# Forget gates' logits and softplus: from the front of the softmax attention into the last chunk of the input projection

## The chip, the cores and the metric

The kernel runs on one core of one Trainium2 chip. The metric is the device time of one execution in microseconds; the median of several runs counts. A core has five engines that run their own instruction queues in order and meet through semaphores: TensorE (matrix products and transposes, into the eight banks of PSUM), VectorE, ScalarE, GpSimd and SyncE, which here starts nearly all DMA transfers.

## The reference, cut to what matters

Two layers of one transformer block (the first block) are followed by one layer of another, on 512 tokens of width 1024 in float32. The change touches the first block's attention, which runs twice. For each layer:

```python
h = rms_norm(x, attn_pre_g[l])
proj = h @ w_in[l]                      # 1024 -> 3080 columns
qa, ka, va, qb, kb, vb, f_logit = jnp.split(proj, split_at, axis=-1)   # 6 x 512 and 8 columns
...                                     # rotary on qa, ka; differential attention on qa, ka, va
log_f = jax.nn.log_sigmoid(f_logit.astype(f32) + forget_bias[l].astype(f32))
ob = forgetting_attention(qb, kb, vb, log_f)
# in it: c = jnp.cumsum(log_f, axis=1); logits = q k / 8 + (c_q - c_k), causal softmax, times v
```

log_sigmoid(y) is computed as min(y, 0) - ln(1 + exp(-|y|)). The 8 columns f_logit are the "logits" of this document, ln(1 + exp(-|y|)) its softplus, and c its running sums.

## The kernel before, in words

**Number format.** A float32 product is made of three fp32r matmuls: operands are split into a rounded part (`_hi`) and the rest (`_lo`), and `three` (lines 1793 to 1797) issues hi x hi, hi x lo and lo x hi. ScalarE rounds each 1024 x 512 piece of weights (`hi_lap`, line 742), GpSimd subtracts to get the rest (`lo_lap`, line 649), and SyncE loads the raw piece (line 547). A weight chunk is 1024 rows by 512 columns, held in four slots of 256 rows (r = 0 to 3). TensorE counts the semaphore `w_used` up when it is through with a slot; ScalarE may then write the next chunk's rounded weights there.

**The input projection.** The stage is named `in0` or `in1` after its layer and has six chunks of 512 output columns: qa, ka, va, qb, kb, vb. Chunk c writes banks 0 to 3 of PSUM when c is even and banks 4 to 7 when it is odd. One slot of one chunk is 2 x 4 x 3 = 24 matmuls of 512 columns (`use_slot` in `token_chunk`). VectorE copies each finished chunk out of PSUM (line 1341, chunk 5 at line 1339) and counts `evac[c % 2]` up, on which TensorE waits before it writes these banks again. On TensorE chunks 0 and 1 are straight code; chunks 2 to 5 are a hardware loop of two passes over two chunks each (`pe.Fori` in `project`, line 1948).

**The front of the attention** (`attention1`, one function of this name on ScalarE, line 859, VectorE, line 1332, and TensorE, line 2040). TensorE's order is: the 16 logit matmuls (lines 2046 and 2047, 16 stationary columns: the 8 forget columns' rounded part and rest) into bank 0, once chunk 4 has been copied out; the wait for chunk 5's copy (`evac[1]`); then 16 items of four 128 x 128 transposes each (line 2037), which turn the heads' q and k and use banks 2 to 7 in rotation. Items with an even number are taken out of PSUM by ScalarE (line 854), those with an odd one by VectorE (line 1371), and an item waits for the one that stood in its bank six items earlier. Between items 1 and 2 TensorE turns the logits back to tokens on partitions, with four small transposes (line 2056) into bank 1, after ScalarE has copied them from bank 0 (line 867). VectorE adds the bias and the two parts (lines 1364 and 1365) ahead of item 3, ScalarE does Abs, Exp and Ln (lines 872 to 874) ahead of item 4, and VectorE makes the gate (line 1368) ahead of item 9. After item 15 TensorE waits for the last items on both engines and for the gate, then makes the running sums (lines 2067 and 2069) and begins with the attention's score products (line 2102).

**What sets the order.** Everything is written out by hand: each engine's queue is in the order of the code, and semaphores tie them. ScalarE's queue at this place is: the rounding of the six chunks' weights, the rounding of the out projection's first four slots (`hi_first(f"out{l}")`, each waits for chunk 5 to be through with the slot), the copy of the logits, and then the items.

Of the kernel before, what the change touches and what calls it, by code (L numbers as in the profile page):

```python
# [170 lines left out]
def build(nc, x, positions, attn_pre_g, w_in, forget_bias, lam_q1, lam_k1, lam_q2, lam_k2, diff_sub_g,  # L171
# [4 lines left out]
    with ctx:  # L176
# [545 lines left out]
        def _(act):  # L722
# [3 lines left out]
            def link(ins):  # L726

                steps[0] += 1
                ins.then_inc(act_step, 1)
                act.wait_ge(act_step, steps[0])  # L730
# [13 lines left out]
            def hi_first(stage, slots=range(R)):  # L744

                hi_lap(stage, LAP0[stage], 0, FFN_SEEN.get(stage), slots)
# [112 lines left out]
            def attention1(l):  # L859
                stage = f"in{l}"  # L860

                with act.Fori(2 if l == 0 else 1, LAPS[stage]) as lap:
                    hi_lap(stage, LAP0[stage] + lap)
                hi_first(f"out{l}")

                act.wait_ge(f_mm, l + 1)
                nc.scalar.activation(f_rows, PS[0:16, 0, :], ACT.Copy).then_inc(f_copied, 1)

                for n, item in enumerate(items1):
                    if n == 4:  # L870
                        act.wait_ge(f_biased, l + 1)
                        link(nc.scalar.activation(fy[:, 1], fy[:, 0], ACT.Abs))
                        link(nc.scalar.activation(fy[:, 1], fy[:, 1], ACT.Exp, scale=-1.0))
                        nc.scalar.activation(fy[:, 1], fy[:, 1], ACT.Ln, bias=1.0).then_inc(f_log, 1)
                    if n % 2 == 0:
                        act.wait_ge(tr_mm, len(items1) * l + n + 1)
                        turned_out(item, 2 + n % 6).then_inc(tr_act, 1)
# [296 lines left out]
        def _(dve):  # L1174
# [157 lines left out]
            def attention1(l):  # L1332
                stage = f"in{l}"
                dst = (QA, KA, VA, QB, KB, None)
                for c in range(6):
                    chunk_done(stage, c)
                    src = banks(c % 2)
# [22 lines left out]
                for n, (src, rows, to, scale) in enumerate(items1):  # L1360
                    if n == 3:
                        dve.wait_ge(f_turned, l + 1)
                        parts = PS[:, 1, 0:T * 16].rearrange("p (t h) -> p t h", h=16)
                        link(V.tensor_tensor(fy[:, 0], parts[:, :, 0:8], fbias[:, l, :].unsqueeze(1).to_broadcast([P, T, 8]), ALU.add))
                        V.tensor_tensor(fy[:, 0], parts[:, :, 8:16], fy[:, 0], ALU.add).then_inc(f_biased, 1)
                    if n == 9:
                        dve.wait_ge(f_log, l + 1)
                        V.scalar_tensor_tensor(fy[:, 2], fy[:, 0], 0.0, fy[:, 1], ALU.min, ALU.subtract).then_inc(f_gate, 1)
                    if n % 2:
                        dve.wait_ge(tr_mm, len(items1) * l + n + 1)  # L1370
                        V.tensor_scalar(to, PS[0:rows, 2 + n % 6, :], scale, None, ALU.mult).then_inc(tr_dve, 1)
# [418 lines left out]
        def _(pe):  # L1790
# [96 lines left out]

            def token_chunk(stage, lap, s, laps, first, next_stage=None, tiled=False):

# [4 lines left out]
                for lap3 in range(laps):  # L1894
                    for r, subs in enumerate(lap_subs(stage, lap3)):
# [3 lines left out]
                        for sub in range(subs):  # L1899
# [7 lines left out]
                            if sub == subs - 1:  # L1907
                                last.then_inc(w_used, 1)
                            if first and not is_down(stage):
                                transposed_next(stage, k)  # L1910
# [19 lines left out]
                for r in range(R):  # L1930
# [6 lines left out]
                    last.then_inc(w_used, 1)  # L1937

            def project(stage):

                n = LAPS[stage]
                for c in range(2):
# [3 lines left out]
                    else:  # L1946
                        token_chunk(stage, LAP0[stage] + c, c, 1, c == 0)
                with pe.Fori(1, n // 2) as i:
                    for s in range(2):
                        pe.wait_ge(evac[s], SET0[stage][s] + i)  # L1950
                        token_chunk(stage, LAP0[stage] + 2 * i + s, s, 1, False)
                if n % 2:
# [87 lines left out]
            def attention1(l):  # L2040
                stage = f"in{l}"

                pe.wait_ge(evac[0], SET0[stage][0] + 3)
                pe.wait_ge(fw_done, 1)
                for k in range(KD):
                    mm(PS[0:16, 0, :], fw[:, l, k, :], xt_hi[:, k, :], start=k == 0, stop=False)
                    last = mm(PS[0:16, 0, :], fw[:, l, k, :], xt_lo[:, k, :], start=False, stop=k == KD - 1)
                last.then_inc(f_mm, 1)
                pe.wait_ge(evac[1], SET0[stage][1] + 3)
                base = len(items1) * l  # L2050
                for n in range(8):
                    if n == 2:

                        pe.wait_ge(f_copied, l + 1)
                        for t in range(T):
                            last = nc.tensor.transpose(PS[:, 1, 16 * t:16 * t + 16], f_rows[:, t * P:(t + 1) * P],
                                                       ident[0:16, 0:16])
                        last.then_inc(f_turned, 1)
                    transpose_item(n, base, items1, 2 + n % 6, 6)
                for n in range(8, len(items1)):  # L2060
                    transpose_item(n, base, items1, 2 + n % 6, 6)
# [326 lines left out]
```

## Time and profile before

| what | value |
|---|---|
| three runs | 2107.34 us median, 2105.56 to 2108.14 |
| the profiled execution's own time | 2107.81 us |
| its span, first to last instruction | 2106.0 us |
| granted TensorE clock, mean | 0.997 |
| TensorE busy | 2061.6 us, 98% of the span |
| VectorE busy | 1146.7 us, 54% |
| ScalarE busy | 915.1 us, 43% |
| GpSimd busy | 598.2 us, 28% |

The busy time of an engine is the time in which it has an instruction in work; TensorE's matmuls overlap each other, so that the start of one to the start of the next is the time that a matmul costs in a row of them, and the duration shown for one is longer than that. The profile is of one execution, and times in its rows count from its first instruction.

### The profile page before, as it was taken

To read this page: it belongs to the slowest core of one execution; us is meant where nothing else is said; L and a number is where in the kernel's file an instruction comes from. 1 tells how busy PE (TensorE), PEld (TensorE's weight loads), DVE (VectorE), ACT (ScalarE), POOL (GpSimd) and SP (SyncE) were. 2 spreads that over 40 slices of the span, in tenths; PEclk is the share of its full clock that TensorE was granted. 3 is DMA by queue.
4 is the path that set the end of the run, shared out by engine and by line. 5 is a ranking of instruction groups with operands and counts; after the bars stand their busy time and mean duration, and the time that the engine had idled before them with its cause. 6 is when DMAs were issued, how large, how long until landed. Compare 5 with 4: busy or idle time off the path is not lost.

```text
span 2106.0 us, 31405 instructions
## 1 busy us (share of the span) xinstructions
PE 2061.6 (98%) x12462; PEld 1795.2 (85%) x12462; DVE 1146.7 (54%) x1784; ACT 915.1 (43%) x1556; POOL 598.2 (28%) x438
## 2 busy tenths in 40 slices
PE   7999999999999999999999999999999999999999
PEld 6886789999887886789999887877788889999987
DVE  6417558776305117558776306477566445877700
ACT  4226454455324126454455325455534434545611
POOL 3540030000544440030000543444466441000252
PEclk9999999999999999999999999999999999999999
DMA  5330023332323330023332331211211232333232
GB/s 193 100 110 1 2 90 104 98 121 91 112 94 98 98 100 1 1 90 103 99 120 91 110 95 55 82 59 50 61 51 51 101 100 81 101 101 111 86 114 72
DMA packets 129143, 178.80 MB, mean 85 GB/s; under 512 B 10163, under 2 KB 78062, under 8 KB 129006
## 3 DMA queue, kind: packets, MB, share of 16 engines
q1 hardware_dynamic: 128414, 175.24, 26.3%
q8 instruction: 96, 1.57, 0.3%
q10 hardware_dynamic: 592, 1.64, 0.2%
q14 instruction: 41, 0.34, 0.1%
HBM read 174.76 MB, written 2.10 MB: 84 GB/s over the span
## 4 chain that ended last, share of the span: by engine, by line
PE 42%; issue 42%; POOL 7%; DVE 6%; ACT 2%; DMA 0%; POOLq 0%; DVEq 0%; ACTq 0%
PE PS L1795 10%; PE PS L1797 10%; PE PS L1796 10%; POOL w_lo L649 7%; PE PS L2127 2%; PE PS L2102 2%; PE PS L2247 1%; PE PS L2086 1%; DVE nmax L1403 1%; PE PS L2037 1%; PE PS L2223 1%; PE PS L2215 1%; PE PS L1849 1%; PE PS L2109 0%; DVE R L1413 0%
## 5 line engine op out<-in xcount | busy, mean ns | idle before, releaser
L649 POOL TENSOR_TENSOR w_lo<-R,w_hi 128x1024 fp32r<-128x1024 f32 x168 | 404.4, 2416 | 1184.9 <-ACT w_hi L742 1125.7
L1795 PE MATMUL PS<-w_hi,xt_hi 128*128 128x512 f32 x928 | 375.3, 404 | 10.6 <-DVE R L1604 4.3
L1795 PE MATMUL PS<-xt_hi,w_hi 128*128 128x256 f32 (+1 forms) x1216 | 367.3, 302 | 0.0
L742 ACT ACTIVATE w_hi<-R 128x1024 fp32r<-128x1024 f32 (+1 forms) x180 | 183.4, 1029 | 423.2 <-PE PS L1797 422.8
L1797 PE MATMUL PS<-w_hi,xt_lo 128*128 128x512 f32 x928 | 364.3, 393 | 0.0
L1796 PE MATMUL PS<-w_lo,xt_hi 128*128 128x512 f32 x928 | 363.5, 392 | 0.0
L1797 PE MATMUL PS<-xt_hi,w_lo 128*128 128x256 f32 (+1 forms) x1216 | 361.8, 298 | 0.0
L1796 PE MATMUL PS<-xt_lo,w_hi 128*128 128x256 f32 (+1 forms) x1216 | 361.6, 297 | 0.0
L1796 PEld LDWEIGHTS PS<-xt_lo,w_hi 128*128 128x128 f32 x1216 | 233.0, 192 | 6.9 <-issue 1.0
L1795 PEld LDWEIGHTS PS<-xt_hi,w_hi 128*128 128x128 f32 x1216 | 233.0, 192 | 7.0 <-issue 1.0
L1797 PEld LDWEIGHTS PS<-xt_hi,w_lo 128*128 128x128 f32 x1216 | 232.9, 192 | 6.5
L1795 PEld LDWEIGHTS PS<-w_hi,xt_hi 128*128 128x128 f32 x928 | 175.5, 189 | 48.4 <-issue 6.8
L1795 PE MATMUL PS<-w_hi,ht_hi 128*128 128x512 f32 x528 | 206.5, 391 | 1.2 <-POOL w_lo L649 0.8
L1797 PEld LDWEIGHTS PS<-w_hi,xt_lo 128*128 128x128 f32 x928 | 175.2, 189 | 37.7
L1796 PE MATMUL PS<-w_lo,ht_hi 128*128 128x512 f32 x528 | 205.7, 390 | 0.0
L1797 PE MATMUL PS<-w_hi,ht_lo 128*128 128x512 f32 x528 | 205.6, 389 | 0.0
L1796 PEld LDWEIGHTS PS<-w_lo,xt_hi 128*128 128x128 f32 x928 | 175.8, 189 | 33.7 <-issue 1.0
L1484 DVE TENSOR_TENSOR w_lo<-UF,w_hi 128x1024 fp32r<-128x1024 f32 x108 | 131.9, 1221 | 52.3 <-ACT w_hi L950 52.3
L633 POOL TENSOR_TENSOR w_lo<-raw,w_hi 128x256 fp32r<-128x256 f32 x160 | 119.7, 779 | 118.3 <-ACT w_hi L1030 75.0
L950 ACT ACTIVATE w_hi<-UF 128x1024 fp32r<-128x1024 f32 x108 | 113.2, 1051 | 29.4 <-PE PS L1797 29.4
L1797 PE MATMUL PS<-UR,w_lo 128*128 128x256 f32 x432 | 122.4, 283 | 0.0
L1796 PE MATMUL PS<-UR,w_hi 128*128 128x256 f32 x432 | 122.4, 283 | 0.0
(299 smaller groups left out, 3546.2 us busy)
## 6 DMA issues: line engine op xcount, KB each, us to landing
R<-in_w_in SPq DMA_DIRECT2D x56, 512.0 KB, 3.8
R<-in_w_down SPq DMA_DIRECT2D x40, 512.0 KB, 3.4
UW<-in_w_gate SPq DMA_DIRECT2D x36, 512.0 KB, 4.0
UW<-in_w_up SPq DMA_DIRECT2D x36, 512.0 KB, 5.0
raw<-in_w_in SPq DMA_DIRECT2D x36, 512.0 KB, 3.7
R<-in_w_out SPq DMA_DIRECT2D x24, 512.0 KB, 3.3
R<-in_w_ffn_down SPq DMA_DIRECT2D x20, 512.0 KB, 3.4
UW<-in_w_ffn_gate SPq DMA_DIRECT2D x18, 512.0 KB, 4.0
```

Of the source, the lines that this page charges most:

```text
L633: last = nc.gpsimd.tensor_tensor(w_lo[:, r, n // 2, cols], raw[:, r, n // 2, cols], w_hi[:, r, n // 2, cols].bitcast(F32), ALU.subtract)
L649: nc.gpsimd.tensor_tensor(w_lo[:, r, 0:subs, :], raw_of(stage, lap)[:, r, 0:subs, :], w_hi[:, r, 0:subs, :].bitcast(F32), ALU.subtract).th ...
L742: nc.scalar.activation(w_hi[:, r, 0:subs, :], raw_of(stage, lap)[:, r, 0:subs, :], ACT.Copy).then_inc(hi_ready, 1)
L950: nc.scalar.activation(slot_hi[slot], src, ACT.Copy).then_inc(u_hi, 1)
L1403: V.tensor_reduce(nmax[:, bank:bank + 2], PS[:, bank:bank + 2, 0:P * (i + 1)], AX.X, ALU.max, negate=True).then_inc(max_done, 2)
L1484: V.tensor_tensor(slot_lo[slot], src, slot_hi[slot].bitcast(F32), ALU.subtract).then_inc(u_lo, 1)
L1795: mm(out_, a_hi, b_hi, start=start, stop=False, **kw)
L1796: mm(out_, a_hi, b_lo, start=False, stop=False, **kw)
L1797: return mm(out_, a_lo, b_hi, start=False, stop=stop, **kw)
L1849: last = nc.tensor.transpose(PS[:, half_bank(stage, half, k), a:a + P], SOURCE[stage][:, 2 * half + t, k * P:(k + 1) * P], ident[:, :])
L2102: mm(PS[:, u % 4 + m, 0:upto], q[halves[m], pair, upto - P:upto], kk[halves[m], pair, 0:upto], start=True, stop=False)
L2127: last = mm(PS[:, 6 + n % 2, 0:width], probT[:, n % 2, j * P:(j + 1) * P], vals, start=j == 0, stop=j == i)
```

## The change

The same instructions are issued in another order, with one loop of TensorE written out.

- TensorE: the logit matmuls and the small transposes become functions of their own (`forget_logits`, `forget_turned`). `token_chunk` gets an argument `between`, which calls them behind slot 1 and behind slot 2 of chunk 5. For this chunks 2 to 5 of both input projections are straight code instead of a loop. `attention1` begins with the wait for chunk 5's copy and issues the 16 items without interruption.
- ScalarE: the copy of the logits and Abs, Exp and Ln stand ahead of the rounding of the out projection's first four slots, and no longer behind it and among the items.
- VectorE: bias, sum and gate stand ahead of the wait for chunk 5, and no longer among the items.
- The running sums stay behind the items.

```diff
@@ -861,17 +861,15 @@
 
                 with act.Fori(2 if l == 0 else 1, LAPS[stage]) as lap:
                     hi_lap(stage, LAP0[stage] + lap)
-                hi_first(f"out{l}")
-
                 act.wait_ge(f_mm, l + 1)
                 nc.scalar.activation(f_rows, PS[0:16, 0, :], ACT.Copy).then_inc(f_copied, 1)
+                act.wait_ge(f_biased, l + 1)
+                link(nc.scalar.activation(fy[:, 1], fy[:, 0], ACT.Abs))
+                link(nc.scalar.activation(fy[:, 1], fy[:, 1], ACT.Exp, scale=-1.0))
+                nc.scalar.activation(fy[:, 1], fy[:, 1], ACT.Ln, bias=1.0).then_inc(f_log, 1)
+                hi_first(f"out{l}")
 
                 for n, item in enumerate(items1):
-                    if n == 4:
-                        act.wait_ge(f_biased, l + 1)
-                        link(nc.scalar.activation(fy[:, 1], fy[:, 0], ACT.Abs))
-                        link(nc.scalar.activation(fy[:, 1], fy[:, 1], ACT.Exp, scale=-1.0))
-                        nc.scalar.activation(fy[:, 1], fy[:, 1], ACT.Ln, bias=1.0).then_inc(f_log, 1)
                     if n % 2 == 0:
                         act.wait_ge(tr_mm, len(items1) * l + n + 1)
                         turned_out(item, 2 + n % 6).then_inc(tr_act, 1)
@@ -1333,6 +1331,13 @@
                 stage = f"in{l}"
                 dst = (QA, KA, VA, QB, KB, None)
                 for c in range(6):
+                    if c == 5:
+                        dve.wait_ge(f_turned, l + 1)
+                        parts = PS[:, 1, 0:T * 16].rearrange("p (t h) -> p t h", h=16)
+                        link(V.tensor_tensor(fy[:, 0], parts[:, :, 0:8], fbias[:, l, :].unsqueeze(1).to_broadcast([P, T, 8]), ALU.add))
+                        V.tensor_tensor(fy[:, 0], parts[:, :, 8:16], fy[:, 0], ALU.add).then_inc(f_biased, 1)
+                        dve.wait_ge(f_log, l + 1)
+                        V.scalar_tensor_tensor(fy[:, 2], fy[:, 0], 0.0, fy[:, 1], ALU.min, ALU.subtract).then_inc(f_gate, 1)
                     chunk_done(stage, c)
                     src = banks(c % 2)
                     if c == 5:
@@ -1358,14 +1363,6 @@
                         rotary(dst[c])
 
                 for n, (src, rows, to, scale) in enumerate(items1):
-                    if n == 3:
-                        dve.wait_ge(f_turned, l + 1)
-                        parts = PS[:, 1, 0:T * 16].rearrange("p (t h) -> p t h", h=16)
-                        link(V.tensor_tensor(fy[:, 0], parts[:, :, 0:8], fbias[:, l, :].unsqueeze(1).to_broadcast([P, T, 8]), ALU.add))
-                        V.tensor_tensor(fy[:, 0], parts[:, :, 8:16], fy[:, 0], ALU.add).then_inc(f_biased, 1)
-                    if n == 9:
-                        dve.wait_ge(f_log, l + 1)
-                        V.scalar_tensor_tensor(fy[:, 2], fy[:, 0], 0.0, fy[:, 1], ALU.min, ALU.subtract).then_inc(f_gate, 1)
                     if n % 2:
                         dve.wait_ge(tr_mm, len(items1) * l + n + 1)
                         V.tensor_scalar(to, PS[0:rows, 2 + n % 6, :], scale, None, ALU.mult).then_inc(tr_dve, 1)
@@ -1885,7 +1882,7 @@
                         if half == 1:
                             last.then_inc(w_used, 1)
 
-            def token_chunk(stage, lap, s, laps, first, next_stage=None, tiled=False):
+            def token_chunk(stage, lap, s, laps, first, next_stage=None, tiled=False, between=None):
 
                 a_hi, a_lo = (ht_hi, ht_lo) if is_down(stage) else (xt_hi, xt_lo)
                 kn = KF if is_down(stage) else KD
@@ -1906,6 +1903,8 @@
                                             k == 0, k == kn - 1)
                             if sub == subs - 1:
                                 last.then_inc(w_used, 1)
+                                if between and r in between:
+                                    between[r]()
                             if first and not is_down(stage):
                                 transposed_next(stage, k)
                             k += 1
@@ -1936,6 +1935,23 @@
                     last = tile_product(3, r, k0[r], k0[r] == 0)
                     last.then_inc(w_used, 1)
 
+            def forget_logits(l):
+
+                pe.wait_ge(evac[0], SET0[f"in{l}"][0] + 3)
+                pe.wait_ge(fw_done, 1)
+                for k in range(KD):
+                    mm(PS[0:16, 0, :], fw[:, l, k, :], xt_hi[:, k, :], start=k == 0, stop=False)
+                    last = mm(PS[0:16, 0, :], fw[:, l, k, :], xt_lo[:, k, :], start=False, stop=k == KD - 1)
+                last.then_inc(f_mm, 1)
+
+            def forget_turned(l):
+
+                pe.wait_ge(f_copied, l + 1)
+                for t in range(T):
+                    last = nc.tensor.transpose(PS[:, 1, 16 * t:16 * t + 16], f_rows[:, t * P:(t + 1) * P],
+                                               ident[0:16, 0:16])
+                last.then_inc(f_turned, 1)
+
             def project(stage):
 
                 n = LAPS[stage]
@@ -1945,10 +1961,11 @@
                         chunk_by_half(stage, 0)
                     else:
                         token_chunk(stage, LAP0[stage] + c, c, 1, c == 0)
-                with pe.Fori(1, n // 2) as i:
-                    for s in range(2):
-                        pe.wait_ge(evac[s], SET0[stage][s] + i)
-                        token_chunk(stage, LAP0[stage] + 2 * i + s, s, 1, False)
+                l = int(stage[-1])
+                for c in range(2, n):
+                    pe.wait_ge(evac[c % 2], SET0[stage][c % 2] + c // 2)
+                    hooks = {1: lambda: forget_logits(l), 2: lambda: forget_turned(l)} if c == n - 1 else None
+                    token_chunk(stage, LAP0[stage] + c, c % 2, 1, False, between=hooks)
                 if n % 2:
                     set_free(stage, n - 1, 0)
                     token_chunk(stage, LAP0[stage] + n - 1, 0, 1, False)
@@ -2040,24 +2057,9 @@
             def attention1(l):
                 stage = f"in{l}"
 
-                pe.wait_ge(evac[0], SET0[stage][0] + 3)
-                pe.wait_ge(fw_done, 1)
-                for k in range(KD):
-                    mm(PS[0:16, 0, :], fw[:, l, k, :], xt_hi[:, k, :], start=k == 0, stop=False)
-                    last = mm(PS[0:16, 0, :], fw[:, l, k, :], xt_lo[:, k, :], start=False, stop=k == KD - 1)
-                last.then_inc(f_mm, 1)
                 pe.wait_ge(evac[1], SET0[stage][1] + 3)
                 base = len(items1) * l
-                for n in range(8):
-                    if n == 2:
-
-                        pe.wait_ge(f_copied, l + 1)
-                        for t in range(T):
-                            last = nc.tensor.transpose(PS[:, 1, 16 * t:16 * t + 16], f_rows[:, t * P:(t + 1) * P],
-                                                       ident[0:16, 0:16])
-                        last.then_inc(f_turned, 1)
-                    transpose_item(n, base, items1, 2 + n % 6, 6)
-                for n in range(8, len(items1)):
+                for n in range(len(items1)):
                     transpose_item(n, base, items1, 2 + n % 6, 6)
                 pe.wait_ge(tr_act, (base + len(items1)) // 2)
                 pe.wait_ge(tr_dve, (base + len(items1)) // 2)
```

## Rows read from the trace of the kernel before

**Rows 1.** The page, part 1: busy us (share of the span) and instructions.
```profile
PE 2061.6 (98%) x12462; PEld 1795.2 (85%) x12462; DVE 1146.7 (54%) x1784; ACT 915.1 (43%) x1556; POOL 598.2 (28%) x438
```

**Rows 2.** Waits of TensorE, whole span: us in total, times, longest.
```profile
PE PS L2067 <- ACT R L854: 1.7, 2, 0.8
```

**Rows 3.** Timeline of layer 0: start us, us, engine, line, what, count [idle before <-releaser].
```profile
149.63 0.39 PE L1797 MATMUL PS<-w_hi,xt_lo 128*128 128x512 f32 x1
...
150.06 2.29 DVE L1339 COPY R<-PS 128x2048 f32<-128x2048 f32 x1 [19.47 <-PE PS L1797]
...
151.25 2.40 POOL L649 TENSOR_TENSOR w_lo<-R,w_hi 128x1024 fp32r<-128x1024 f32 x1 [3.04 <-ACT w_hi L742]
...
153.33 0.39 PE L2047 MATMUL PS<-xt_lo,fw 128*16 128x512 f32 x1
...
153.56 1.03 PE L2037 MATMUL PS<-ident,R 128*128 128x128 f32 x8
153.76 0.59 ACT L867 ACTIVATE R<-PS 16x512 f32<-16x512 f32 x1 [2.58 <-PE PS L2047]
...
154.53 0.42 PE L2056 MATMUL PS<-ident,R 16*128 16x16 f32 x4
...
154.88 6.33 PE L2037 MATMUL PS<-ident,R 128*128 128x128 f32 x56
155.25 0.18 DVE L1364 TENSOR_TENSOR fy<-PS,fbias 128x32 f32<-128x32 f32 x1
...
156.06 0.22 ACT L872 ACTIVATE fy<-fy 128x32 f32<-128x32 f32 x1
...
158.36 0.18 DVE L1368 SCALAR_TENSOR_TENSOR fy<-fy 128x32 f32<-128x32 f32 x1
...
161.25 0.69 DVE L1371 TENSOR_SCALAR R<-PS 128x512 f32<-128x512 f32 x1 [0.18 <-PE PS L2037]
...
162.04 0.38 PE L2067 MATMUL PS<-fy,sums_r 128*128 128x32 f32 x2 [0.83 <-ACT R L854]
```

**Rows 4.** The same timeline at the same place of layer 1.
```profile
781.53 0.39 PE L1797 MATMUL PS<-w_hi,xt_lo 128*128 128x512 f32 x1
...
781.96 2.29 DVE L1339 COPY R<-PS 128x2048 f32<-128x2048 f32 x1 [19.47 <-PE PS L1797]
...
785.47 1.04 PE L2037 MATMUL PS<-ident,R 128*128 128x128 f32 x8
```

**Rows 5.** Timeline at the loop's back edge, chunk 3 to chunk 4, layer 0.
```profile
106.11 0.39 PE L1797 MATMUL PS<-w_hi,xt_lo 128*128 128x512 f32 x1
...
106.34 0.39 PE L1795 MATMUL PS<-w_hi,xt_hi 128*128 128x512 f32 x1
...
106.54 2.29 DVE L1341 COPY R<-PS 128x2048 f32<-128x2048 f32 x1 [17.55 <-PE PS L1797]
```

**Rows 6.** Timeline: matmuls that follow transposes within a projection's chunk.
```profile
651.02 0.48 PE L1795 MATMUL PS<-w_hi,xt_hi 128*128 128x512 f32 x1
...
651.34 0.39 PE L1796 MATMUL PS<-w_lo,xt_hi 128*128 128x512 f32 x1
```

**Rows 7.** Stretches: length, busy us (instructions) of each engine, PEclk, DMA share, GB/s.
```profile
153.50:162.00 8.50, 7.71 (x69) 7.21 (x67) 5.92 (x11) 5.71 (x12) 0.16 (x1) 1.00 0.20 64
...
164.70:168.10 3.40, 3.40 (x12) 1.41 (x12) 2.18 (x6) 1.89 (x8) 0.00 (x0) 0.50 0.00 0
...
1506.10:1512.90 6.80, 4.99 (x14) 3.55 (x13) 4.50 (x3) 1.59 (x2) 4.84 (x4) 0.50 0.00 0
...
640.00:646.00 6.00, 4.66 (x25) 3.67 (x25) 2.67 (x8) 4.94 (x10) 4.57 (x2) 1.00 0.26 86
```

**Rows 8.** Timeline of TensorE at three places behind idle time.
```profile
9.45 1.94 PE L1849 MATMUL PS<-ident,R 128*128 128x128 f32 x8 [4.24 <-DVE R L1202]
...
643.82 1.09 PE L1849 MATMUL PS<-ident,R 128*128 128x128 f32 x8 [1.34 <-DVE R L1202]
...
1505.45 0.50 PE L1795 MATMUL PS<-w_hi,xt_hi 128*128 128x512 f32 x1 [2.03 <-DVE R L1604]
```

## The prediction, made before the changed kernel was run

> **What bounds the kernel now.** I read the busy shares on the page first. TensorE is busy for 2061.6 of 2106.0 us, so a change earns time only if it shortens TensorE's instruction stream or its waits [rows 1]. The second view is TensorE's table of waits. At the place of the change it knows one kind of wait only: 1.7 us over both layers, at the running sums on line 2067, for the last turned head pair to leave PSUM (it names ScalarE; the timeline shows VectorE's evacuation ending last) [rows 2]. The third view, the timeline, gives the order of the work around it in layer 0 [rows 3]. Behind the projection's last matmul (start 149.63) TensorE goes straight on with the 16 forget-logit matmuls, the last of which starts at 153.33, and then with the first 8 transposes at 153.56. Under the logits, and this is the row to look at, VectorE copies chunk 5 out of PSUM from 150.06 to 152.35. The transposes wait for that copy, but it has been over for 1.2 us when they are due, so the wait costs nothing. Layer 1 repeats this to within 0.01 us [rows 4], so every cost below counts twice.
>
> **The change part by part.**
>
> *Logits moved ahead of slots 2 and 3.* The 16 matmuls cost (153.56 - 149.63 - 0.23) = 3.70 us of TensorE, 0.23 us each, at either place; the matmuls next to them are also 0.23 us apart [rows 3, 5]. Their work is neither added nor removed. The two waits that come with them are over before: bank 0 was copied out under chunk 5's first slot (chunk copies take 2.29 us, a slot is 24 matmuls of 0.227 = 5.4 us), and the converted forget weights date from the start of the kernel. In layer 0 the logits now stand 10.9 us ahead of the chunk's end.
>
> *What they covered is bare.* Chunk 5's last matmul is now the last thing before the head pairs' transposes, which still wait for chunk 5's copy. The copy starts 0.43 us behind the start of the last matmul (150.06 - 149.63) and lasts 2.29 us. TensorE restarts 0.10 us behind such a release (161.25 + 0.69 = 161.94 to 162.04) or 0.18 us (ScalarE's 153.76 + 0.59 = 154.35 to 154.53); I take 0.14 [rows 3]. From last matmul to first transpose that is 0.43 + 2.29 + 0.14 = 2.86 us, where now one step of 0.23 us stands between two instructions. So TensorE loses 2.63 us in each layer. Bounds: 2.59 and 2.67 us. Nothing else is in TensorE's queue that could pass this wait, since it is ahead of all the transposes on an in-order queue.
>
> *Turned logits moved between slots 2 and 3.* In the kernel before they interrupt the transposes: 8 transposes of 0.109 us would end 0.87 us behind 153.56, and the next run starts at 154.88, so the interruption with its wait for ScalarE's copy costs 1.32 - 0.87 = 0.45 us. At the new place ScalarE has 5.4 us for its 0.59 us copy, so the wait is gone; the four small transposes are 0.35 us, and a matmul behind transposes takes 0.32 us to its successor and not 0.23 (651.02 to 651.34) [rows 3, 6]. 0.35 + 0.09 = 0.44: nothing gained, between 0 and 0.1 us per layer either way.
>
> *Bias, Abs, Exp, Ln and the gate.* They run on VectorE and ScalarE. From the last small transpose (about 154.8) to the end of Ln about 2.0 us pass now (biases at 155.25, three ScalarE steps of 0.25 us from 156.06), with a head pair's evacuation in between. At the new place that chain and the gate (0.18 us) need some 2 us and have slot 3's 5.4 us as cover. VectorE is then back at its wait for chunk 5 with over 3 us to spare; without the cover each microsecond of lateness would be one of TensorE. Taking them out of the transposes gives nothing: those run at TensorE's own step, 56 in 6.10 us, and the running sums wait for the last evacuation (161.94), not for the gate, which was ready at 158.54 [rows 3]. That 0.83 us wait stays as it is and is what comes late next.
>
> *ScalarE's roundings of the out projection's first weights* now queue behind Ln. Three of 1.06 us fit between Ln and the end of the chunk or just behind it, while ScalarE has no transpose to evacuate for 2.9 us. GpSimd's four subtractions of 2.40 us bunch behind them and run over the copy and the transposes. In the trace one of them already lies over chunk 5's copy from 151.25, and that copy took the 2.29 us of the others [rows 3, 5]: no charge. SyncE's four loads of the next weights wait for those subtractions and start up to 10 us later; their data are needed only behind the attention, which begins then. No charge.
>
> *Loop unrolled.* TensorE's loop over chunks 2 to 5 becomes straight code. Its back edge lies between the matmuls at 106.11 and 106.34, where chunk 3's copy (106.54) shows the chunk's end. The step is 0.23 us as everywhere, so nothing is saved here [rows 5]. The Trainium skill, "Runtime: NRT & Kernel Launch", section "Instruction fetch mechanics", says that a taken branch to a target outside the fetched window stalls the engine until it is loaded, and prefers unrolling. By that rule unrolling would gain; the row at the back edge shows no stall, so its sum stands only among the rivals.
>
> *TensorE's clock.* The granted clock was 1.00 in the whole of 153.50:162.00, though TensorE did nothing but transposes there. It was 0.50 (1.2 GHz) in 1506.10:1512.90, behind a wait of 2.03 us, and in 164.70:168.10, behind the 0.83 us wait and small matmuls; an idle stretch of 1.34 us at 643.82 left it at 1.00 [rows 7, 8]. The new idle stretch (about 2.5 us) is nearest to the one of 2.03 us, so a fall is to be expected in part of the executions. At the lower level 8 transposes take 1.94 us and not 1.09 [rows 8], about double per step. A stretch as long as the 3.40 us of 164.70:168.10 at half speed loses 1.7 us of transposes at most, and less where it begins while TensorE still waits. Bounds for the two layers: 0 and 3.4 us; I take the middle, 1.7 us.
>
> **The sum.** 2 x 2.63 = 5.3 us of bare copy, 0 for the rest, 1.7 us for the clock: +7.0 us. The profiled execution took 2107.81 us (span 2106.0 and 1.8 around it), which gives 2114.8; it lies 0.47 us above the median of the runs shown, 2107.34, so the forecast for a median is 2114.3. Its own range is 2107.34 + 4.7 to + 8.9 with half a microsecond either way for the spread of the runs: 2111.6 to 2116.7.
>
> **The rivals.**
>
> 1. *The clock does not come back under transposes.* All 64 transposes of each layer run at 1.2 GHz: 64 x (0.213 - 0.109) = 6.7 us per layer, 13.3 in all, 2107.34 + 5.3 + 13.3 = 2125.9. For it: no row shows the clock rising while TensorE only transposes; the 8 at 9.45 stay low. Against it: 8.5 us of transposes kept the high level [rows 7]. The Trainium skill, "TensorE: Matmul & The Clock Gate", Part 4, says that transposes do not count as busy for the clock in the same way; the kept level at 153.50:162.00 speaks against its strong form. 10%.
>
> 2. *The other side: the loop was paid for after all.* If entry and back edge of the loop cost TensorE time that the modelled starts do not show, unrolling returns it: 4 such places (two layers, entry and back edge). To come out within 0.2% (4.2 us) it must return over 2.8 us of the 7.0, 0.7 us each, as much as the larger waits of this stage; to make the kernel faster by over 0.2% it must return 11.2 us, 2.8 us each. From 1.75 us each the change is no longer slower at all: 2107.3. For it: only the rule of the Trainium skill named above. Against it: the 0.23 us step at the back edge [rows 5]. 10%, of which 3% for faster.
>
> 3. *The chain is late.* If the gate's chain took more than slot 3 (5.4 us), VectorE's copy of chunk 5 would start late and TensorE wait longer still. The chain would have to be 3.4 us longer than the trace shows, as when ScalarE is held by something queued ahead of it; a microsecond behind that is 2 us over both layers, so about 2118. Against it: ScalarE's queue is empty there once chunk 5's weights are rounded. 5%.
>
> **How the numbers follow.** The forecast has 75%, the rivals 10, 10 and 5. A measurement of this kernel tells about 0.2%, 4.2 us, from no change. The forecast's low end of +4.2 touches that, where a copy is released a little earlier or the before kernel's median lies higher on the measuring chip: 3 of its 75 count as "same", with 7 of rival 2. Faster 0.03, same 0.10, slower 0.87. The range reaches down into rival 2 and up to rival 3: 2110.6 to 2118.5; rival 1 and most of rival 2 stay outside.
>
> **What would show it.** In the changed kernel's timeline a wait of TensorE on VectorE's chunk-5 copy (line 1339 before) of 2.4 to 2.6 us ahead of the first head pair, in both layers; the logits in the middle of chunk 5 with steps of 0.23 us around them; no wait for the turned logits; Ln ended before chunk 5's last matmul; the wait at the running sums unchanged at 0.8 us; GpSimd over the first transposes and no VectorE evacuation longer than 0.69 us; and the granted clock just behind the new wait, 1.00 or 0.50. The prediction is wrong if no such wait appears, if the transposes take longer than 7 us at a clock of 1.00, or if something else than this stage moves.

## The result and the profile after

The changed kernel takes 2113.61 us in the median of 8 runs (2112.12 to 2115.46), the kernel before 2107.03 us in 8 runs beside it (2105.34 to 2108.14). The ratio is 1.0034, with a 95% interval of 1.0025 to 1.0043: 6.6 us slower, where 7.0 us slower was forecast (2114.3, 2110.6 to 2118.5). The profiled execution took 2115.11 us.

Part 1 of the changed kernel's page answers to [rows 1].

```profile
PE 2062.7 (98%) x12462; PEld 1796.1 (85%) x12462; DVE 1147.0 (54%) x1784; ACT 915.1 (43%) x1556; POOL 597.7 (28%) x438
```

TensorE has the same 12462 matmuls and only 1.1 us more busy time, in a span that is 6.7 us longer. So the time is mostly idling. TensorE's table of waits has one entry that [rows 2] do not know, and the old one beside it, unchanged (us in total, times, longest):

```profile
PE PS L2054 <- DVE R L1344: 4.8, 2, 2.4
...
PE PS L2069 <- ACT R L854: 1.7, 2, 0.8
```

Line 2054 holds the items' transposes and line 1344 chunk 5's copy. The timeline of layer 0 shows the place; it answers to [rows 3].

```profile
147.96 0.39 PE L1794 MATMUL PS<-w_hi,xt_lo 128*128 128x512 f32 x1
148.27 0.41 PE L1951 MATMUL PS<-ident,R 16*128 16x16 f32 x4
148.62 0.50 PE L1792 MATMUL PS<-w_hi,xt_hi 128*128 128x512 f32 x1
148.73 0.19 DVE L1337 TENSOR_TENSOR fy<-PS,fbias 128x32 f32<-128x32 f32 x1 [18.09 <-PE PS L1951]
...
148.95 0.40 PE L1793 MATMUL PS<-w_lo,xt_hi 128*128 128x512 f32 x1
...
149.70 0.23 ACT L869 ACTIVATE fy<-fy 128x32 f32<-128x32 f32 x1
149.84 2.94 ACT L742 ACTIVATE w_hi<-R 128x1024 fp32r<-128x1024 f32 x3
...
150.96 9.36 POOL L649 TENSOR_TENSOR w_lo<-R,w_hi 128x1024 fp32r<-128x1024 f32 x4 [19.08 <-ACT w_hi L742]
...
153.99 0.39 PE L1794 MATMUL PS<-w_hi,xt_lo 128*128 128x512 f32 x1
154.41 2.29 DVE L1344 COPY R<-PS 128x2048 f32<-128x2048 f32 x1 [4.26 <-PE PS L1794]
154.47 1.06 ACT L742 ACTIVATE w_hi<-R 128x1024 fp32r<-128x1024 f32 x1 [1.69 <-PE PS L1794]
156.76 8.87 PE L2054 MATMUL PS<-ident,R 128*128 128x128 f32 x64 [2.38 <-DVE R L1344]
...
157.89 0.69 DVE L1368 TENSOR_SCALAR R<-PS 128x512 f32<-128x512 f32 x1 [1.19 <-PE PS L2054]
...
166.46 0.38 PE L2069 MATMUL PS<-fy,sums_r 128*128 128x32 f32 x2 [0.83 <-ACT R L854]
```

The chain of the logits is over early: Ln ends at 149.93 and VectorE is back at its wait for chunk 5 4.3 us before that is due. What follows the last projection matmul (153.99) is the copy alone, and TensorE stands until 156.76. The same place of layer 1 answers to [rows 4]:

```profile
791.08 2.29 DVE L1344 COPY R<-PS 128x2048 f32<-128x2048 f32 x1 [4.26 <-PE PS L1794]
...
793.43 7.21 PE L2054 MATMUL PS<-ident,R 128*128 128x128 f32 x64 [2.38 <-DVE R L1344]
```

The wait is the same, but the 64 transposes take 8.87 us in layer 0 and 7.21 us in layer 1. The table of stretches names the reason (length, busy us of TensorE, its weight loads, VectorE, ScalarE, GpSimd, granted clock, DMA share, GB/s); it answers to [rows 7].

```profile
156.80:157.80 1.00, 1.00 (x10) 1.00 (x10) 0.00 (x0) 0.35 (x1) 1.00 (x1) 1.00 0.86 182
157.90:161.30 3.40, 3.40 (x18) 3.40 (x17) 1.53 (x3) 1.34 (x3) 2.42 (x2) 0.50 0.66 243
161.40:165.60 4.20, 4.20 (x39) 4.00 (x37) 3.20 (x5) 2.75 (x5) 0.00 (x0) 1.00 0.36 125
168.20:171.50 3.30, 3.30 (x14) 1.69 (x14) 1.76 (x5) 1.77 (x8) 0.00 (x0) 0.50 0.02 5
...
793.40:800.50 7.10, 7.07 (x64) 6.97 (x64) 4.84 (x7) 4.45 (x8) 3.61 (x2) 1.00 0.67 222
```

In layer 0 the granted clock was 0.50 (1.2 GHz) for 3.4 us from 1.1 us behind the end of the wait, and fell again in the attention's first products; in layer 1 it did neither. It was back at 1.00 (2.4 GHz) with nothing but transposes on TensorE. From start to start a transpose took 0.213 us at 0.50 and 0.109 us at 1.00; 16 of them fell into the low stretch, which makes 16 x 0.104 = 1.66 us.

The start of an execution shifts by up to 1.5 us from one to the next, so times of two traces are compared from a mark. The mark here is the last transpose that feeds the projection (32.77 and 664.68 in the kernel before). Starts behind it, in us, read off the timelines of the profiled executions; the rows below the second are kernels of the experiments further down:

| kernel | first item, both layers | running sums, layer 0 / 1 | first transpose of the out projection, layer 0 / 1 |
|---|---|---|---|
| before | 120.79 | 129.27 / 129.27 | 212.71 / 212.85 |
| changed | 123.94 | 133.64 / 131.97 | 217.49 / 214.72 |
| loop written out | 120.79 | 129.27 / 129.26 | 213.01 / 211.99 |
| 10 matmuls in the wait | 123.94 | 131.98 / 131.97 | 214.72 / 214.72 |
| two items ahead | 121.40 | 131.10 / 131.10 | 213.84 / 213.83 |
| four items ahead | 121.40 | 130.23 / 130.24 | 212.97 / 212.99 |
| copy twice | 126.26 | 136.55 / 136.44 | 219.31 / 219.18 |
| only TensorE's part | 123.94 | 133.64 / 133.63 | 216.38 / 216.35 |
| before, sums first | 120.80 | 128.29 / 128.27 | 211.05 / 211.02 |
| four items and sums first | 121.40 | 129.24 / 129.23 | 212.03 / 212.02 |
| before, wait filled | 120.79 | 129.27 / 129.26 | 212.03 / 212.02 |

Without a clock fall the running sums start 2.70 us later than before (131.97 against 129.27), with one 4.37 us. From the sums to the out projection it is 82.75 us without a fall (changed kernel, layer 1) and 83.4 to 83.9 with one; the kernel before had one in both layers of its profile. So the two profiles differ by 4.78 us in layer 0 and by 1.87 us in layer 1, 6.65 in all, and under 0.2 us is left for the rest of the kernel. That this agrees with the 6.6 us of the medians is in part chance: the profiled executions had clock falls that many others did not have, as is counted behind the experiments.

### The profile page after: what moved, and what is told of

Same layout as the page of the kernel before. It is cut to its first block, busy times and chain, and to the rows that moved or that the text cites. A ratio compares the mean times of both kernels' runs of the same rounds, so it can differ in the third digit from the quotient of the medians.

```text
span 2112.7 us, 31367 instructions
## 1 busy us (share of the span) xinstructions
PE 2062.7 (98%) x12462; PEld 1796.1 (85%) x12462; DVE 1147.0 (54%) x1784; ACT 915.1 (43%) x1556; POOL 597.7 (28%) x438
## 4 chain that ended last, share of the span: by engine, by line
PE 42%; issue 41%; POOL 7%; DVE 7%; ACT 2%; DMA 0%; POOLq 0%; DVEq 0%; ACTq 0%
PE PS L1792 10%; PE PS L1794 10%; PE PS L1793 10%; POOL w_lo L649 7%; PE PS L2129 2%; PE PS L2104 2%; PE PS L2249 1%; PE PS L2088 1%; DVE nmax L1400 1%; PE PS L2054 1%; PE PS L2225 1%; PE PS L2217 1%; PE PS L1846 1%; PE PS L2111 0%; PE PS L1798 0%
```

## The experiments

The theory is that TensorE waits for a copy that its logits used to cover, and that the clock takes more in part of the executions. Each kernel ran in five rounds beside the kernel before.

**Only the loop written out** (kernel before):

```diff
-                with pe.Fori(1, n // 2) as i:
-                    for s in range(2):
-                        pe.wait_ge(evac[s], SET0[stage][s] + i)
-                        token_chunk(stage, LAP0[stage] + 2 * i + s, s, 1, False)
+                for c in range(2, n):
+                    pe.wait_ge(evac[c % 2], SET0[stage][c % 2] + c // 2)
+                    token_chunk(stage, LAP0[stage] + c, c % 2, 1, False)
```

> The kernel before with TensorE's loop over chunks 2 to 5 of both input projections written out, and nothing else. Main theory (the whole +6.6 us is chunk 5's copy laid bare plus a clock fall behind the wait): unrolling is worth nothing, 2107.0 us, within 0.7 us of before, because the matmul step at the back edge was 0.23 us already. Rival (the loop was paid for, and unrolling hides part of a larger loss): 2 to 4 us faster than before. Second rival (longer straight code costs instruction fetch): 1 to 6 us slower than before.

Measured: 2106.59 us, before 2106.58; ratio 1.0000 (0.9991 to 1.0009). To the first item and to the sums the trace has the same times as before, to 0.01 us (table above). So the loop cost nothing and its removal brings nothing. Rival 2 of the prediction, which needs 2.8 us or more, is out, and so is a cost of longer code beyond the interval's 1.9 us. The Trainium skill ("Runtime: NRT & Kernel Launch", "Instruction fetch mechanics") has a taken branch stall the engine when its target is outside what is fetched; for TensorE at this back edge neither the step [rows 5] nor this pair of times shows a stall, and no trace tells whether this target was outside.

**Useless matmuls in the wait** (changed kernel):

```diff
+                for n in range(10):
+                    mm(PS[0:16, 0, :], fw[:, l, n % KD, :], xt_hi[:, n % KD, :], start=True, stop=True)
                 pe.wait_ge(evac[1], SET0[stage][1] + 3)
```

> The changed kernel with 10 useless logit matmuls (results overwritten later, 10 x 0.23 = 2.3 us) in front of the wait for chunk 5's copy, in both layers. They fit into the 2.63 us that TensorE idles, so the wait itself ends when it did. Main theory: the idle stretch costs twice, by its length and by the clock fall that follows it in part of the executions; with the idling filled the fall is gone and the time is that of the quicker executions of the changed kernel, 2112.3 us, 1.0 to 1.7 us below its median of 2113.6, with less scatter than its 3.3 us. Rival (the clock plays no part, the scatter is of other origin): 2113.6 us as the changed kernel. Third possibility (the matmuls are not free): 2114 or more.

Measured: 2111.88 us (2110.98 to 2112.73); ratio 1.0027 (1.0017 to 1.0038). That is 5.3 us above before, near twice the 2.70 us by which the sums start late without a clock fall, and 1.3 us less than the changed kernel's 6.6. The timeline shows the filler:

```profile
153.94 2.49 PE L2061 MATMUL PS<-xt_hi,fw 128*16 128x512 f32 x10
154.15 2.29 DVE L1344 COPY R<-PS 128x2048 f32<-128x2048 f32 x1 [4.26 <-PE PS L1794]
...
156.49 1.75 PE L2054 MATMUL PS<-ident,R 128*128 128x128 f32 x14
```

The transposes begin at the same point behind the mark (123.94) although TensorE now does more, and in this trace the clock does not fall in either layer. The idle stretch therefore has a second price besides its length, and it is the clock's: the 1.67 us of layer 0. The scatter goes from 3.3 to 1.75 us, which says little, since the kernel before scatters by 2.8 us without such a stretch. The two medians come from separate measurements, each against its own runs of before, so 1.3 is uncertain by about a microsecond; the two traces are not.

**Two items ahead of the wait** (changed kernel):

```diff
-                pe.wait_ge(evac[1], SET0[stage][1] + 3)
                 base = len(items1) * l
                 for n in range(len(items1)):
+                    if n == 2:
+                        pe.wait_ge(evac[1], SET0[stage][1] + 3)
                     transpose_item(n, base, items1, 2 + n % 6, 6)
```

> The changed kernel with the wait for chunk 5's copy moved behind items 0 and 1, which only need banks 2 and 3. 8 transposes of 0.109 us then lie under the copy: 0.87 us less idling per layer. Main theory: -1.7 us from the length, up to -1 us more because the shorter idle stretch lets the clock fall less often: 2111.0 to 2111.9 us. Rival (the loss is not TensorE's wait for the copy but something in the placement of the logits within the chunk): 2113.6 us, unchanged.

Measured: 2110.00 us; ratio 1.0017 (1.0008 to 1.0026), 3.4 us above before. The wait is 1.51 us long instead of 2.38. Expected was a gain of 1.7 to 2.6 us on the changed kernel's +6.6; it is 3.2. The gain came out larger than its range. By the traces the length gives 0.87 us per layer, and both falls that the changed kernel's trace has in layer 0, the one behind the wait and the one in the attention, are missing here.

**Four items ahead** (changed kernel):

```diff
-                pe.wait_ge(evac[1], SET0[stage][1] + 3)
                 ...
+                pe.wait_ge(f_biased, l + 1)
                 for n in range(len(items1)):
-                    transpose_item(n, base, items1, 2 + n % 6, 6)
+                    if n == 4:
+                        pe.wait_ge(evac[1], SET0[stage][1] + 3)
+                    transpose_item(n, base, items1, n % 8, 8)
```

(The evacuations use the same banks, and TensorE waits for `f_biased` before it writes bank 1.)

> The changed kernel with items in banks 0 to 7 in rotation (before 2 to 7), so that items 0 to 3 go to banks 0 to 3 and stand ahead of the wait for chunk 5's copy: 16 transposes, 1.75 us under the copy per layer, 0.9 us of idling left. Main theory: -3.5 us from the length and about -1 from the clock: 2109.0 to 2110.1 us, twice the step of the version with two items. Rival (placement within the chunk is what costs): 2113.6 us.

Measured: 2106.93 us; ratio 1.0002 (0.9993 to 1.0011). The waits of the two versions with items ahead, one entry from each table:

```profile
PE PS L2054 <- DVE R L1344: 3.0, 2, 1.5
```

```profile
PE PS L2054 <- DVE R L1344: 1.3, 2, 0.6
```

Each pair of items takes 0.87 us off the wait (2.38, 1.51, 0.64 us) and off the start of the running sums (131.97, 131.10, 130.23). The placement rival is out. The median came out 2 us better than expected. The lengths leave +1.9 us over before, and +0.35 was measured. The trace shows two candidates for the difference: it has no clock fall in the attention, and in a stage that was not edited, near 1507 us and at two waits of some 2 us, the low clock lasted 3.4 us and not the 6.8 us of the kernels before and changed:

```profile
1507.00:1510.20 3.20, 2.81 (x7) 2.24 (x8) 2.65 (x2) 0.00 (x0) 3.20 (x2) 0.50 0.00 0
1510.40:1513.00 2.60, 2.60 (x17) 2.18 (x16) 0.69 (x1) 0.94 (x2) 1.23 (x2) 1.00 0.00 0
```

Which of the two it was is taken up behind the last experiment. Why this kernel should have the low stretch shorter stays open.

**The copy made twice** (changed kernel):

```diff
+                        link(V.tensor_copy(VB[:, :, :, 0:HD], heads(src, 8)))
                         V.tensor_copy(VB[:, :, :, 0:HD], heads(src, 8)).then_inc(evac[1], 1)
```

> The changed kernel with VectorE's copy of chunk 5 made twice, one after the other, in both layers (2.29 us more ahead of TensorE's transposes). Main theory (TensorE waits for this copy and for nothing else there): +2.3 to +2.4 us per layer, and a clock fall behind the wait in nearly all executions instead of in part of them, up to 1.7 us per layer less what the changed kernel has already: 2106.6 + 6.6 + 4.7 = 2117.9 us with the falls as often as now, 2120 us with them always. Rival (the copy's cost is hidden in part behind something else of the same length, such as ScalarE's or GpSimd's bunched work): 2113.2 to 2115.5 us.

Measured: 2120.03 us (2119.32 to 2120.52); ratio 1.0062 (1.0048 to 1.0076), 13.2 us above before, where 13 was expected with falls in every execution. The timeline and two stretches of layer 0:

```profile
153.20 2.29 DVE L1344 COPY R<-PS 128x2048 f32<-128x2048 f32 x1 [4.26 <-PE PS L1795]
155.53 2.29 DVE L1345 COPY R<-PS 128x2048 f32<-128x2048 f32 x1
...
157.87 5.31 PE L2055 MATMUL PS<-ident,R 128*128 128x128 f32 x26 [4.71 <-DVE R L1345]
```

```profile
153.10:155.60 2.50, 0.06 (x1) 0.00 (x0) 2.37 (x2) 1.06 (x1) 2.50 (x2) 1.00 0.61 210
155.80:162.50 6.70, 4.63 (x22) 4.63 (x23) 3.40 (x3) 1.26 (x3) 3.30 (x2) 0.50 0.65 232
```

TensorE's wait grows by just the added copy (2.38 to 4.71 us). The clock falls while TensorE still waits and stays low into the transposes, in both layers. All five runs lie within 1.2 us, and their mean granted clock is 0.995 each time, as in the profiled one: a fall that comes every time does not scatter.

**Only TensorE's part of the change**: logits and small transposes in chunk 5, loop written out, but bias, Abs, Exp, Ln and gate among the items as before.

```diff
-                act.wait_ge(f_biased, l + 1)          # and Abs, Exp, Ln: back ahead of item 4
                 hi_first(f"out{l}")
-                    if c == 5:                        # bias and gate: back ahead of items 3 and 9
-                        dve.wait_ge(f_turned, l + 1)
```

> The changed kernel with TensorE's order as changed, but bias, Abs, Exp, Ln and gate back at their old places among the items on VectorE and ScalarE, and the rounding of the out projection's weights back ahead of them (behind the copy of the logits). So only TensorE's part of the change is made. Main theory (all of the loss is TensorE's order): 2113.2 us, the same as the changed kernel within 0.8 us. Rival (ScalarE's and GpSimd's bunched work or VectorE's chain ahead of its copy carries part of the loss): 2108 to 2111.5 us.

Measured: 2114.03 us in six runs; ratio 1.0031 (1.0018 to 1.0043), 7.2 us above before. Layer 0 of its trace:

```profile
153.89 2.29 DVE L1338 COPY R<-PS 128x2048 f32<-128x2048 f32 x1 [23.77 <-PE PS L1796]
...
155.09 2.36 POOL L649 TENSOR_TENSOR w_lo<-R,w_hi 128x1024 fp32r<-128x1024 f32 x1 [3.63 <-ACT w_hi L742]
...
156.24 8.87 PE L2056 MATMUL PS<-ident,R 128*128 128x128 f32 x64 [2.38 <-DVE R L1338]
```

GpSimd's subtractions no longer bunch over the transposes, the chain is back among the items, and TensorE's wait is the same 2.38 us. So the loss is the changed kernel's; the moved softplus chain, ScalarE's roundings behind it and GpSimd's bunched subtractions have no part in it that these runs could tell. The trace has the fall behind the wait in both layers.

**The other part of the front: sums under the wait** (kernel before):

```diff
-                pe.wait_ge(tr_act, (base + len(items1)) // 2)
-                pe.wait_ge(tr_dve, (base + len(items1)) // 2)
-
+                pe.wait_ge(tr_act, base // 2 + 6)
                 pe.wait_ge(f_gate, l + 1)
                 ...
                 last.then_inc(c_mm, 1)
+                pe.wait_ge(tr_act, (base + len(items1)) // 2)
+                pe.wait_ge(tr_dve, (base + len(items1)) // 2)
```

> The kernel before, logits at their old place, with one edit: the running sums' 8 matmuls stand ahead of the wait for the last evacuations instead of behind it (they wait for the gate and for item 10, which used their bank). They take 0.96 us and the wait is 0.83 us, in both layers. Main theory (the gate is ready early even at the old place, so the sums can move without the logits): -1.7 to -1.9 us from the work laid under the wait, and up to -1.5 us more if the clock falls behind this place less often: 2103.2 to 2104.9 us. Rival (the attention's first products wait for VectorE's decay columns or the evacuation anyway): 2106.6 us, unchanged.

Measured: 2103.04 us; ratio 0.9984 (0.9975 to 0.9993), 3.8 us faster than before, where 1.9 us by length and up to 3.4 with the clock were expected. It beats both kernels. The timeline shows the sums directly behind the transposes and the scores 0.95 us earlier behind the mark than before:

```profile
159.82 0.31 PE L2065 MATMUL PS<-fy,sums_r 128*128 128x32 f32 x2
159.96 0.81 PE L2067 MATMUL PS<-fy,sums_r 128*128 128x24 f32 x6
160.02 0.69 DVE L1371 TENSOR_SCALAR R<-PS 128x512 f32<-128x512 f32 x1 [0.18 <-PE PS L2037]
160.81 0.49 PE L2102 MATMUL PS<-R 64*128 64x128 f32 x4
```

The gate was ready at 158.54 in the kernel before [rows 3]: for this the logits did not have to move. The low clock near 1505 us is short in this trace, as in the kernel with four items:

```profile
1503.60:1506.90 3.30, 3.30 (x8) 2.62 (x9) 2.22 (x1) 0.00 (x0) 3.30 (x3) 0.50 0.00 0
1507.10:1510.00 2.90, 2.90 (x21) 2.47 (x20) 1.00 (x2) 1.19 (x2) 0.69 (x1) 1.00 0.02 6
```

**Both together**: four items ahead and the sums first (items' banks in the order 0, 1, 2, 3, 6, 7, 4, 5, and item 12 as the one whose evacuation the sums await).

```diff
+TURN_BANKS = [0, 1, 2, 3, 6, 7, 4, 5]
-                    transpose_item(n, base, items1, n % 8, 8)
+                    transpose_item(n, base, items1, TURN_BANKS[n % 8], 8)
```

> The changed kernel with four items ahead of the wait for chunk 5's copy, as in the version at 2106.93 us, and with the running sums ahead of the wait for the last evacuations (items' banks reordered to 0, 1, 2, 3, 6, 7, 4, 5, so that the sums' bank is free in time). Main theory: the version with four items less 0.9 us per layer, 2105.0 us, less than the kernel before but more than the kernel before with the same edit, by the 0.8 us of wait left per layer and the dearer placement inside the chunk. Rival (the two edits share one hidden cost, the clock): 2106 to 2107 us.

Measured: 2106.41 us; ratio 0.9998 (0.9989 to 1.0007). Each against its own runs of before (-0.4 and +0.35 us), it is better than four items alone by 0.75 us only, and 1.4 us worse than expected. The time lies in the rival's range, although the trace shows the 0.96 us per layer (212.03 against 212.98 behind the mark). Here the low clock of the untouched stage near 1505 us is 6.8 us long again, and by the two traces the rest of the kernel took up most of the gain: from the second out projection to the end it is 1.3 us longer than in the kernel with four items.

**The old wait filled** (kernel before):

```diff
+                for n in range(3):
+                    mm(PS[0:16, 0, :], fw[:, l, n, :], sums_r[:, 4:8, :], start=True, stop=True)
                 pe.wait_ge(tr_act, (base + len(items1)) // 2)
```

> The kernel before with three useless 512-column matmuls (3 x 0.23 = 0.7 us, result overwritten later) ahead of the 0.83 us wait that stands before the running sums, in both layers. No work is moved and the wait ends when it did, so nothing changes but what TensorE does while it waits. Open from the version with the running sums first: it gained 3.8 us where its lengths explain 1.9 us. Main theory (the other 1.9 us is the clock fall behind this wait, which before has in part of its executions at a price of 0.7 to 1.1 us a layer): 2105.0 to 2106.0 us, 0.7 to 1.7 us under the kernel before. Rival (the surplus is scatter between chips or another effect of the sums' place): 2106.7 us, unchanged.

Measured: 2107.07 us against 2106.49; ratio 1.0002 (0.9993 to 1.0011). This expectation failed. The attention's start has no fall in this trace (212.03 and 212.02 behind the mark, where before has 212.71 and 212.85), but the median is not lower. So that fall does not explain the 1.8 to 1.9 us by which the version with the sums first beats its lengths.

**How often the clock fell.** The record has the mean granted clock of every execution, to three decimals, and the traces say what stands behind a value. At 0.999 (four items, sums first) the only low stretch is one of 3.4 us near 1505 us. At 0.998 it is one of 6.8 us there, alone or with one of 3.4 us elsewhere (loop written out). At 0.997 there are two of 3.4 us beside the 6.8 (before, changed, only TensorE's part), at 0.995 two more of 6.8 (copy twice). Of 67 executions of the kernel before beside the experiments 3 are at 0.999, 51 at 0.998 and 13 at 0.997. So the profile of before, with a fall in both layers, is of the rarer kind, and filling its wait could gain little in a median. Of the changed kernel's eight executions five are at 0.998 (2112.12 to 2113.66 us), and the three at 0.997 or 0.996 are slower than all of them (2114.66 to 2115.46): its scatter goes with the clock.

The next table sets lengths beside medians, both in us against before. The length is twice the delay of the out projection's first transpose against 212.02 behind the mark (before with its wait filled, no fall), read in a layer without a fall:

| kernel | by the lengths | measured | executions at 0.999 | low clock near 1505 us in the trace |
|---|---|---|---|---|
| loop written out | 0.0 | 0.0 | 0 of 11 | 6.8 |
| 10 matmuls in the wait | +5.4 | +5.3 | 1 of 8 | 6.8 |
| two items ahead | +3.6 | +3.4 | 0 of 11 | 6.8 |
| four items ahead | +1.9 | +0.35 | 8 of 11 | 3.4 |
| before, sums first | -2.0 | -3.8 | 7 of 11 | 3.4 |
| four items and sums first | 0.0 | -0.4 | 0 of 11 | 6.8 |
| before, wait filled | 0.0 | +0.6 | 0 of 11 | 6.8 |

Only the two kernels with the short low stretch in a stage that nobody edited miss their lengths by more than 0.6 us. Their executions at 0.998 have medians 1.2 us above before (four items, three executions) and 2.2 us below (sums first, four), nearer to the lengths. So the surplus goes with the executions that had a low clock of 3.4 us near 1505 us and no other. From the second out projection to the end it is 1227.7 and 1227.9 us in these two traces and 1228.2 to 1229.0 in the nine others, so the short stretch accounts for 0.3 to 1.3 us of the 1.6 and 1.8; part of the rest may be attention falls that before has and they do not. What makes the stretch short is not shown.

## Why the prediction was right

- *The bare copy, 2.63 us per layer*: the sums start 2.70 us late where no clock fall is mixed in, and the version with the wait filled measures 5.3 us for both. From last matmul to first transpose it is 2.77 us (2.86 forecast): the release took 0.06 us and not 0.14. So the bare copy costs 2.54 us, just under the stated bounds of 2.59 to 2.67; the other 0.15 us of the 2.70 stand under the next point.
- *Small transposes, 0 net*: this was 0.15 us per layer too low, outside its 0 to 0.1. Between the matmuls at 147.96 and 148.95 lie 0.99 us where two steps of 0.23 stood, 0.53 us, and the next few steps are 0.01 longer. At the old place they cost 0.45. With 0.09 us too much on the copy and its release the two errors nearly cancel, by luck.
- *The chain hidden*: right, with 4.3 us to spare (over 3 forecast); the kernel that left it at its old place is 7.2 us slower all the same. Rival 3 never came up.
- *ScalarE's roundings, GpSimd, SyncE, no charge*: right. Four subtractions of 9.36 us together lie over the copy and the transposes; the copy stays at 2.29 us and VectorE's evacuations at 0.69 us.
- *Loop, no charge*: right, 0.0 us.
- *The wait at the sums unchanged and late next*: right, 0.83 us.
- *The clock, 1.7 us with bounds 0 and 3.4*: one fall of 3.4 us behind the wait costs 1.67 us (133.64 against 131.97), which is the bound per layer. The trace had one in two layers. The measured share is 6.6 - 5.4 = 1.2 us. The middle of the range was a choice: the prediction had no row that said how often the clock falls. It also left out the other side: the attention's fall that the kernel before may have, worth 0.7 to 1.1 us, is missing in layer 1 of the changed kernel's trace and pays a little back there. The sum came out right to 0.4 us partly by luck, since these offset each other. The doubled step was read off the transposes at 9.45, for whose stretch (9.40:11.40) the profile gives a granted clock of 1.00; the step at a granted 0.50 is the 0.213 us of the changed kernel.
- *Rival 1, a clock that stays low under transposes*: out. It came back to 1.00 at 161.3 with only transposes on TensorE. The Trainium skill ("TensorE: Matmul & The Clock Gate", Part 4) says that transposes do not count for the clock as matmuls do; here the clock stayed at 1.00 under fp32 transposes alone and rose to it while only they ran.
- *Two numbers do not follow from their terms*: with the stated bounds the low end of the sum is +5.0 and not +4.7, and one microsecond of lateness in rival 3 makes 2116.3 and not about 2118. Neither decides anything, since 2113.61 lies inside either way.

## What to carry to other kernels

When independent work is moved away from behind a product's last matmul, look at what that work covers: here 3.7 us of matmuls hid a 2.3 us PSUM copy, and moving them saved no instruction. Independent work belongs where TensorE waits, as the running sums under the last evacuations (some 2 us gained by length, 3.8 us measured), and not where it is busy. If a wait must stay, put first behind it only what needs it: each pair of items that went ahead of it took its full 0.87 us off.

## What the runs showed of the hardware

An idle stretch of 2.4 us on TensorE costs its length, and in three of four places (both layers of two traces, the changed kernel's and the one with only TensorE's part) a fall of the granted clock to 0.50 for 3.4 us behind it, 1.67 us of dense transposes each time. At 4.7 us of idling the five runs agreed to 1.2 us, and the trace has 6.8 us of low clock in each layer; at 1.5 us and 0.6 us before the same transposes the traces had none. The length of the idling does not decide alone: at the running sums, behind a wait of 0.83 us and small matmuls, the clock fell in 4 of 16 places in eight traces.

Two of the edits in the attention moved the medians by 1.6 to 1.8 us more than their lengths do, and both have in their traces a low clock of 3.4 us instead of 6.8 near 1505 us, some 700 us behind the last edited place. What decides between the two lengths was not settled.
